# Two gated up stages: norm applied behind the matmuls, shift carried as two operand columns, four conditioning tiles in another stage

## The reference, cut to what matters

```python
mod = c_act @ w_ada[l] + b_ada[l]
sh1, sc1, g1, sh2, sc2, g2, sh3, sc3, g3 = jnp.split(mod, N_MOD, axis=-1)
u = modulate(rmsnorm_2(h, norm_ff1[l]), sh1, sc1)        # x*(1+sc) + sh
h = h + FFN_RES * g1 * swiglu(u, w_ff1_gate, w_ff1_up, w_ff1_down)
...                                                       # token mixing with sh2, sc2, g2
u = modulate(rmsnorm_2(h, norm_ff2[l]), sh3, sc3)
h = h + FFN_RES * g3 * swiglu(u, w_ff2_gate, w_ff2_up, w_ff2_down)

def swiglu(x, w_gate, w_up, w_down):
    return (jax.nn.silu(x @ w_gate) * (x @ w_up)) @ w_down
```

## Time and profile before

| | us |
|---|---|
| median of 3 runs | 1440.85 |
| lowest and highest | 1439.37, 1440.9 |
| span of the profiled execution | 1437.8 |
| PE busy in it | 1411.5 (98%) |
| DVE busy | 1111.5 (77%) |
| ACT busy | 690.4 (48%) |

### The profile page before, as it was taken

How to read it: one execution, slowest core, us unless ns; L and a number is a source line. 1 busy time by engine, 2 the same in 40 slices (tenths; PEclk the granted TensorE clock), 3 DMA queues, 4 the chain that set the end, 5 groups by cost and what they waited for, 6 DMA issues and landing times.

```text
span 1437.8 us, 21872 instructions
## 1 busy us (share of the span) xinstructions
PE 1411.5 (98%) x8580; PEld 1243.6 (86%) x8580; DVE 1111.5 (77%) x1660; ACT 690.4 (48%) x899; POOL 33.1 (2%) x21
## 2 busy tenths in 40 slices
PE   7999999999999999999999999999999999999997
PEld 6878998888889888888888988888988889888887
DVE  3799876698767887758887779997578678798664
ACT  2221664455434654645563355553454447555442
POOL 0000000000000000000000000000024100000000
PEclk9999999999999999999999999999999999999999
DMA  7444663355686456525558747757553436475451
GB/s 265 144 167 153 251 214 123 118 186 208 236 292 207 169 188 219 183 94 182 191 204 279 268 179 273 272 188 260 203 204 135 169 103 226 159 273 205 135 179 66
DMA packets 60150, 279.31 MB, mean 194 GB/s; under 512 B 6590, under 2 KB 8063, under 8 KB 35232
## 3 DMA queue, kind: packets, MB, share of 16 engines
q1 hardware_dynamic: 56248, 270.69, 53.7%
q10 hardware_dynamic: 3816, 7.45, 1.5%
HBM read 273.89 MB, written 4.19 MB: 193 GB/s over the span
## 4 chain that ended last, share of the span: by engine, by line
PE 84%; DVE 8%; DMA 5%; ACT 1%; issue 1%; DVEq 0%; SPq 0%; ACTq 0%
PE acc L477 34%; PE acc L479 17%; PE acc L498 10%; DMA ada_w<-in_ada 5%; PE acc L536 3%; PE acc L538 3%; PE acc L537 3%; DVE wsplit L1753 2%; PE acc L636 2%; PE stat L721 2%; DVE ada_w L2142 2%; PE acc L640 1%; PE turned L741 1%; PE stat L833 1%; PE score L1054 1%
## 5 line engine op out<-in xcount | busy, mean ns | idle before, releaser
L477 PE MATMUL acc<-hA,wsplit 128*128 128x512 f32 x1664 | 589.9, 399 | 4.4 <-DVE tsum L1767 1.7
L1176 ACT ACTIVATE wsplit<-raw 128x2048 fp32r<-128x2048 f32 (+3 forms) x214 | 381.2, 1783 | 195.3 <-PE acc L479 145.1
L1753 DVE TENSOR_TENSOR wsplit<-raw,wsplit 128x2048 fp32r<-128x2048 f32 (+3 forms) x214 | 455.1, 2130 | 16.4 <-ACT wsplit L1176 16.4
L479 PE MATMUL acc<-hA,wsplit 128*128 128x256 f32 x1664 | 463.9, 279 | 0.0
L477 PEld LDWEIGHTS acc<-hA,wsplit 128*128 128x128 f32 x1664 | 312.3, 188 | 81.6 <-issue 4.1
L479 PEld LDWEIGHTS acc<-hA,wsplit 128*128 128x128 f32 x1664 | 313.4, 188 | 0.4
L477 PE MATMUL acc<-hid,wsplit 128*128 128x512 f32 x648 | 224.9, 390 | 0.0
L479 PE MATMUL acc<-hid,wsplit 128*128 128x256 f32 x648 | 182.7, 282 | 0.0
L1186 ACT ACTIVATE lowp<-acc 128x512 f32<-128x512 f32 (+1 forms) x118 | 69.0, 585 | 202.8 <-PE acc L479 174.9
L477 PEld LDWEIGHTS acc<-hid,wsplit 128*128 128x128 f32 x648 | 121.6, 188 | 25.6
L479 PEld LDWEIGHTS acc<-hid,wsplit 128*128 128x128 f32 x648 | 122.5, 189 | 0.0
(11 more groups left out here) (315 smaller groups left out, 2051.6 us busy)
## 6 DMA issues: line engine op xcount, KB each, us to landing
raw<-in_gu SPq DMA_DIRECT2D x44, 1024.0 KB, 4.9
ada_w<-in_ada SPq DMA_DIRECT2D x144, 256.0 KB, 4.8
raw<-in_up SPq DMA_DIRECT2D x32, 1024.0 KB, 4.9
raw<-in_down SPq DMA_DIRECT2D x32, 1024.0 KB, 5.0
raw<-in_dn SPq DMA_DIRECT2D x32, 704.0 KB, 4.1
raw<-in_pw SPq DMA_DIRECT2D x12, 1024.0 KB, 8.1
raw<-in_memk SPq DMA_DIRECT2D x8, 1024.0 KB, 4.8
raw<-in_memv SPq DMA_DIRECT2D x8, 1024.0 KB, 5.3
```

The costliest lines, as they stand in the source:

```text
L477: nc.tensor.matmul(dst.rearrange("p (s t) -> p s t", s=2), w, h, start=start, stop=False, skip_group_check=True)
L479: return nc.tensor.matmul(dst[:, 0:T], lo_w, h[:, 0, :], start=False, stop=stop, skip_group_check=True)
L1176: nc.scalar.activation(wsplit[:, slot, 0, 0:elems_of(n)], raw[:, slot, 0:elems_of(n)], ACT.Copy).then_inc(S("w_hi"), 1)
L1753: V.tensor_tensor(wsplit[:, slot, 1, 0:e], raw[:, slot, 0:e], wsplit[:, slot, 0, 0:e].bitcast(F32), ALU.subtract).then_inc(S("w_lo"), 1)
```

## The change

Both gated up stages join the ones whose norm is put off. The shift can't be left to the end as the root can (it isn't multiplied by the root), so each operand tile gets two more columns that hold the shift: high at 256 and 257, low likewise. Tiles have a pitch of 516 instead of 512 values (`PITCH`), and the low half starts at column 258 (`LOW_AT`). The matmuls of `gu1` and `gu2` become three of 258 columns into the same columns of PSUM (`shifted_cols`), so that column 256 of the accumulator is the shift's contribution, one value for each output feature. `total` is then one DVE multiply of PSUM by the root, with 1.0 as the root of that column; ACT's copy to `lowp` falls away (`WHOLE`). The column is added as a scalar: as the bias of the sigmoid, and in the two DVE multiplies of `gated`. For `ffa` the last pair's weighted squares are made on DVE (`weigh`), and PE's sums with them all come last. `gain_sq` shrinks to one column a tile. The four conditioning tiles at `gu1` chunks 3, 7, 11 and 15 go to `dn1` chunks 1, 3, 5 and 7, so `dn1` has one at each of its first eight chunks. All other stages that read `hA` read it at the new pitch.

```diff
+LOW_AT = T + 2
+PITCH = 2 * LOW_AT
-WHOLE = ["branch"]
+WHOLE = ["branch", "gu1", "gu2"]
+SHIFTED = {"gu1": ("ffa", 0), "gu2": ("ffb", 6)}
+LATE = {**DEFERRED, **{stage: norm for stage, (norm, _) in SHIFTED.items()}}
-TILED_OPERANDS = ["memq0", "ff0", "ff1"]
+TILED_OPERANDS = ["memq0", "ff0", "ff1", "ffa", "ffb"]
-SINGLE = ["fox", "ffa", "mixn", "ffb"]
+SINGLE = ["fox", "mixn"]
-    ("down1", range(14)), ("gu1", range(17)), ("dn1", (0, 2, 4, 6)), ...
+    ("down1", range(14)), ("gu1", (0, 1, 2, 4, 5, 6, 8, 9, 10, 12, 13, 14, 16)), ("dn1", range(8)), ...
...
-        hA = place("hA", [P, KT, 2 * T], F32R)
+        operand = place("operand", [P, KT, PITCH], F32R)
...
+            def shifted_cols(slot, par, kts, start, stop, ready):
+                for i, kt in enumerate(kts):
+                    ...
+                    for j in range(2):
+                        at, dst = kt * 2 * P + j * P, acc[:, par, j, 0:LOW_AT]
+                        w, lo_w = wsplit[:, slot, 0, at:at + P], wsplit[:, slot, 1, at:at + P]
+                        nc.tensor.matmul(dst, w, wide[:, kt, 0:LOW_AT], ...)
+                        nc.tensor.matmul(dst, w, wide[:, kt, LOW_AT:PITCH], ...)
+                        mm = nc.tensor.matmul(dst, lo_w, wide[:, kt, 0:LOW_AT], ...)
...
-                        if (c, p) == (1, 0) and name in DEFERRED:
-                            norm_sums(DEFERRED[name], [PAIRS - 2, PAIRS - 1])
+                        if (c, p) == (1, 0) and name in LATE:
+                            norm_sums(LATE[name], [LAST] if LATE[name] == "ffa" else [LAST - 1, LAST])
...
-                if norm in DEFERRED.values():
+                if norm in LATE.values():
                     return
                 norm_sums(norm, range(len(early), PAIRS - 1))
                 norm_sums(norm, [LAST], filler=10)
                 if norm != "final2":
                     keep_clock(40)
...
+            def shift_hi(gu):                                    # ACT
+                ...
+                nc.scalar.activation(wide[:, :, T:T + 2], shift.unsqueeze(2).to_broadcast([P, KT, 2]),
+                                     ACT.Copy).then_inc(S("shift_hi"), 1)
...
+                if st.name in SHIFTED:                           # DVE, total
+                    wait("chunk_done", a + (st.base + 1))
+                    V.tensor_tensor(tsum_wide[:, par, :, 0:T + 1], acc[:, par, :, 0:T + 1],
+                                    spread(rstd_wide[:, 0:T + 1], 2), ALU.mult).then_inc(S("acc_summed"), 1)
+                    return
...
-                    V.tensor_tensor(t0, t0, t1, ALU.mult).then_inc(S(f"{gu}_p"), 1)
+                    V.scalar_tensor_tensor(out=t0, in0=t0, scalar=tsum_wide[:, par, 0, T:T + 1], in1=aux[:, par, 0, :],
+                                           op0=ALU.add, op1=ALU.mult).then_inc(S(f"{gu}_p"), 1)
...
-            feed_forward("up1", "down1")
             wait("mod_used", 2)
-            norm("ffa", x, [(hA, modulated(1))], shift=0)
+            feed_forward("up1", "down1", operand=("ffa", hA, modulated(1)), ahead=lambda: shift_lo("gu1"))
...
-            add_to_x("out", modulated(5))
             wait("mod_used", 5)
-            norm("ffb", x, [(hA, modulated(7))], shift=6 * SEGMENT)
+            shift_lo("gu2")
+            add_to_x("out", modulated(5), operand=("ffb", hA, modulated(7)))
```

More of the change, by code:

```diff
@@ L189 @@
     (f"fox{n}", range(1)) for n in ("k1", "q1", "v1", "k2", "q2", "v2", "k3", "q3", "v3")] + [
-    ("down1", range(14)), ("gu1", range(17)), ("dn1", (0, 2, 4, 6)), ("incols", range(3)), ("ingates", (1, 2, 3)),
+    ("down1", range(14)), ("gu1", (0, 1, 2, 4, 5, 6, 8, 9, 10, 12, 13, 14, 16)), ("dn1", range(8)), ("incols", range(3)), ("ingates", (1, 2, 3)),
     ("gu2", range(8))]
@@ L612, in body @@
                                         q % 2 == 0, q % 2 == 1, ready)
+                    elif name in SHIFTED:
+                        mm = shifted_cols(slot, par, kt_all, begins, ends, ready)
                     elif st.kind == "cols":
@@ L711, in norm_sums @@
                         stat_read(q)
-                    if name == "ffa" and p == first:
-                        pe.wait_ge(S("gain_sq"), 2)
                     for j in range(2):
@@ L723, in norm_sums @@
                                               skip_group_check=True)
-                        if name == "ffa":
-                            weights = ones[:] if p == first else gain_sq[:, 2 * p + j, :]
-                            squares = lowp[:, j, :] if p == first else aux[:, at, j, :]
-                            mm = nc.tensor.matmul(stat[:, 1, :], weights, squares,
-                                                  start=False, stop=p == PAIRS - 1 and j == 1, skip_group_check=True)
+                    if name == "ffa" and p == LAST:
+                        pe.wait_ge(S("weighted"), PAIRS)
+                        for j in range(2):
+                            mm = nc.tensor.matmul(stat[:, 1, :], ones[:], lowp[:, j, :], start=False, stop=j == 1,
+                                                  skip_group_check=True)
                     mm.then_inc(S("norm_stat"), 1)
@@ L1645, in _ @@
             feed_forward("up1")
-            for kt in range(KT):
-                last = nc.scalar.activation(gain_sq[:, kt, :], ones[:], ACT.Square, scale=col("final1", kt))
-            last.then_inc(S("gain_sq"), 1)
+            nc.scalar.activation(gain_sq[:], col("final1", 0, KT), ACT.Square).then_inc(S("gain_sq"), 1)
             wait("gain_sq", 1)
             nc.scalar.activation(gain_sq[:], gain_sq[:], ACT.Identity, bias=col("rms_eps")).then_inc(S("gain_sq"), 1)
-            residual("down1", "ffa", [hA], shift=0)
+            shift_hi("gu1")
+            residual("down1", "ffa", [hA])
             gated_feed_forward("gu1")
@@ L1732, in _ @@
             split_hi(st, st.chunks - 1 + RING, st.chunks - 1 + RING)
-            residual("out", "ffb", [hA], shift=6 * KT)
+            shift_hi("gu2")
+            residual("out", "ffb", [hA])
             gated_feed_forward("gu2")
@@ L1907, in weigh @@
                         for j in range(2):
-                            squares, weight = aux[:, q % 2, j, :], gain_sq[:, 2 * q + j, 0:1]
+                            squares, weight = aux[:, square_at("ffa", q), j, :], gain_sq[:, 2 * q + j:2 * q + j + 1]
                             if q == 0:
```

235 lines of the change are left out of this document (142 added, 93 removed).

## The result

The changed kernel takes 1442.51 us (median of 20 runs, 1441.13 to 1445.44), the one before 1440.34 beside it (20 runs); the ratio is 1.002, with an interval of 1.0014 to 1.0026. I had forecast 1431.5 and a range that ended at 1439.5. The 20 runs lie in two groups, twelve of 1441.13 to 1443.03 and eight of 1444.15 to 1445.44; the profiled execution, with a span 5.0 us longer than that of the earlier trace rows, is one of the eight.

What follows compares the result with a forecast made beforehand. PE was taken as the bound, its work hiding two filled holes at the turns. Turns -6.6 and -3.4, `gu1` -1.1, `dn1` +2.2, `gu2` -0.4 sum to -9.3: 1440.85 to 1431.5 us, range 1425.0 to 1439.5.

Steps and rivals of the forecast that it cites:

- the pace of 258 columns: In `gu1` and `gu2`, three matmuls of 258 columns take 352.5 ns, so a stage takes 124.1 us.
- The bounds of 350.0 and 354.9: Limits on the triple's pace in ns: 350.0 if the extra columns are free, 354.9 at the slower pace `gu2` shows.
- 258 columns are much slower: Rival for the triples of `gu1` and `gu2`: slower than before from 13.3 ns more a triple; chance 0.04.
- What I costed at nothing: Shift's columns on ACT, smaller `gain_sq`, `dn1`'s later tiles, and the pitch of 516 for other readers of `hA`: 0 us.
- the pitch of 516 for the other readers: Rival: about 960 pairs reading `hA` outside the two stages go from 346.7 to 354.9 ns, 7.9 us, 1439.4; chance 0.10.
- `dn1`: With a conditioning tile at every chunk, late loads delay chunk 10's split and PE stalls 2.2 us (0 to 6.4).
- the rule of the Trainium skill: An engine idle between bursts restarts at half clock; applied at `gu2`'s part (1,0), 1.9 us lost, 1433.4; chance 0.05.
- `gu1`'s loop: DVE's conditioning loop of 5.7 us outlasts a 5.55 us chunk in `gu1`; moving tiles gives -1.1 us (-1.9 to 0).
- The turns: Filler matmuls gone and sums moved behind part (1,0): -6.6 us from `down1` to `gu1`, -3.4 from `out` to `gu2`.
- the stand at part (1,0): At the start of `gu2`, PE waits 2.2 us for the last tile's add on DVE.

Runs made afterwards that it cites:

- the blocks: Changed kernel with blocks of 24 triples behind its last matmul, results unread, varying columns and starts; 256 columns at 0, 32 and 64 bytes: 359.6, 350.1, 353.3 ns a triple.
- The table of starts: Blocks added behind the changed kernel's last matmul, varying starts of rows and weights: equal starts 359.6 or 359.7 ns, rows 32 bytes further on 350.1 to 353.3.
- contig: Changed kernel with only the two gated up stages on the wide layout, halves of 1024 bytes for all other readers of `hA`: 1441.23 us.
- ada_only: The kernel before with nothing but the four conditioning tiles moved from the first gated up stage to its down stage: 1442.44 us.

## Why the prediction was wrong

*The step that failed is the pace of 258 columns.* I put six columns at 0.42 ns on the 350.0 of three matmuls of 256 columns: 2.5 ns. I called the 0.42 the slope between that form and 512 + 256, but both have 768 columns, so no slope follows from them. As a size it isn't far off above 258 columns (from 264 to 288 it is 0.46 at a start of 32 and 0.40 at a start of 0), but there is a step at 256. And the 350.0 was itself the pace of one place: `down1` reads `hid` at 32 bytes over, while `operand` begins at a multiple of 128 as `wsplit` does, where the blocks, at a pitch of 2048 bytes, give 360 for 256 columns already. Of the pace measured, 360.0 is what 258 columns take at the start of 32 that had given 350.0, and another 3.3 ns come with the layout of `operand`. 363.3 instead of 352.5 is 10.8 ns, times 704 = 7.6 us. The bounds of 350.0 and 354.9 came from rows that had no matmul between 256 and 512 columns, so they bounded nothing. The rival "258 columns are much slower" had its turning point at 13.3 ns and a chance of 4 in 100; 10.8 is most of the way there.

*What I costed at nothing was 6.1 us in the profile.* I listed the pitch of 516 for the other readers, which is 1.3 us by the run; the 7.9 us of that rival did not come. Its pairs lose 3 ns in `up0` and `up1`. The Trainium skill's note in "SBUF — State Buffer", Door 1: The DMA port swizzle, that each new line pays agrees with the sign; my estimate by it, under 2 ns, was too low. I did not list that a longer tile moves all tiles behind it: 3.1 us by the run. The change shows it in the diff, where three sizes grow and two tiles swap places, and I read that as bookkeeping. By the Trainium skill ("SBUF — State Buffer", Who interferes with whom) PE reads its moving rows and its weights through two independent ports. From that I should have expected, had I asked, that where the one lies doesn't matter to the other. The table of starts shows that it does: 350.1 against 359.6 for the same rows, by the weights' start alone.

*`dn1`* was right in its mechanism, place (a split behind a conditioning tile, an accumulator's adds ahead of it) and nearly in its size: 2.6 us of stand against 2.2. The term was too small by the clock, 1.5 us, and by 0.4 of the slower triples, which belong to the tiles' place. I had gone by the earlier trace rows, where PE stood 1.5 us and the clock stayed, and had weighed the rule of the Trainium skill ("TensorE: Matmul & The Clock Gate", HAM oscillation), that an engine left idle between bursts starts the next one slow, at the turn to `gu2` alone. At part (1,0) of `gu2` the clock did stay; behind the 2.6 us in `dn1` it fell, as that rule has it; in `contig`, behind 2.07 us, it did not. In the median the move costs 1.7.

*`gu1`'s loop* was right: 3.1 us in the kernel before, though about 0.8 of them were not waits but the slower of the two paces behind its stops. But I counted a gain that the slower triples had already made void: once a chunk takes longer than the loop, there is nothing to remove.

*The turns* were right: -7.0 for -6.6 and -4.3 for -3.4; the stand at part (1,0) was 1.07 us, not 2.2, so DVE was less late than I thought.

Put right, the sum is: turns -11.3, triples of `gu1` and `gu2` +5.6 with what their stages had lost before, region +3.1, pitch +1.3, `dn1` and its move +1.7, which is +0.4. The medians say +2.2; the rest is 1.8 us, of which the differences between executions, 0.8 us in the first matmuls and 1.5 us in a stage that falls into the slower pace, may be part; I can't place it.

## What to carry to other kernels

Price a matmul by rows of its own width: between two widths there can be a step. A tile that grows moves every tile behind it, so look up the starts of what the matmuls read before and after, and pad to keep them; here 32 bytes are worth 3 us one way and 5 the other. Compare one stage's pace over several executions before a change is blamed or praised for it. Before a gain is added to a sum, ask whether another term of the same sum has already taken away what it removes.

## What the runs showed of the hardware

- At a pitch of 2048 bytes three matmuls of 256 columns take 359.6 or 359.7 ns in all four blocks where moving rows and weights begin equally far over a multiple of 128 bytes, and 350 to 353 where the rows begin 32 bytes further on, with nothing else running. At a pitch of 2176 bytes it is 356 and 358.
- A triple goes from 350 to 360 ns between 256 and 258 columns where the rows begin 32 bytes over; one matmul of the three is enough (358 to 360). At a start of 0 both take 360.
- Behind PE's stands in `dn1` (idle time in its timeline) the granted clock was 0.50 after 2.48 us (changed kernel) and after 1.85 us (`ada_only`), and 1.00 after 2.07 us (`contig`); after 1.07 us in `gu2` it stayed at 1.00. At 0.50 PE ran for 2.0 us and more.
- Pairs of 512 and 256 columns run at 346.7 or at 353.3 ns in the same stage with the same operands (`gu2`: 353.4 in the kernel before, 346.9 with one norm deferred), and in `up1` at either in two executions of the same instructions. What decides is open.
